# The first norm joined, reciprocals of the softmax sums turned, and three of eight low parts at the FFN heads moved to ScalarE and GpSimd

## The reference

```python
def rms_norm(x, g):
    xf = x.astype(jnp.float32)
    y = xf * lax.rsqrt(jnp.mean(xf * xf, axis=-1, keepdims=True) + EPS)
    return (y * g.astype(jnp.float32)).astype(x.dtype)

def sink_softmax(logits, sink):
    m = jnp.maximum(jnp.max(logits, axis=-1, keepdims=True), sink)
    p = jnp.exp(logits - m)
    return p / (jnp.sum(p, axis=-1, keepdims=True) + jnp.exp(sink - m))

def conv_ffn(x, left, g, w_gate, w_up, cw, cb, w_down):
    xn = rms_norm(x, g)
    a = xn @ w_gate
    ...
    y = (jax.nn.gelu(ac) * (xn @ w_up)) @ w_down
    return y, ap[:, -(CONV_W - 1):]

for i in range(DEPTH):
    ...
    hp = hp + op @ wo                       # mixer, then
    fp, cp = conv_ffn(...)                  # FFN
    hp = hp + fp[:, META:]
```

## Time and profile before

| | |
|---|---|
| median of 3 runs | 2940.51 us (2939.18 to 2941.53) |
| the profiled execution | 2940.25 us, of which 2938.4 are the span of its trace |
| granted TensorE clock, mean | 0.984 of full speed |
| busy, share of the span | PE 97%, PEld 91%, DVE 52%, ACT 23%, POOL 31% |
| first norm and projections of layer 0 | 22 to 174 us |
| attention of layer 0 | 176 to 374 us |
| head of the first FFN (norm m = 1) | 477 to 499 us |
| attention of layer 1 | 1633 to 1955 us |
| head of the second FFN (norm m = 3) | 2057 to 2079 us |

### The profile page before, as it was taken

How to read it: one execution, slowest core, us unless ns; L and a number is a source line. 1 busy time by engine, 2 the same in 40 slices (tenths; PEclk the granted TensorE clock), 3 DMA queues, 4 the chain that set the end, 5 groups by cost and what they waited for, 6 DMA issues and landing times. The chain is left out here.

```text
span 2938.4 us, 48132 instructions
## 1 busy us (share of the span) xinstructions
PE 2854.0 (97%) x18679; PEld 2687.3 (91%) x18679; DVE 1532.0 (52%) x2816; ACT 679.4 (23%) x1327; POOL 918.6 (31%) x860
## 2 busy tenths in 40 slices
PE   8999999999999999999888899999999999999998
PEld 6988899999999999998578777789999999999997
DVE  5046615554444444455588878531644444444455
ACT  4036611000000000003466655631100000000002
POOL 4233333222222222224024754323222222222221
PEclk9999999999999999999999999999999999999999
DMA  4430011111111111114012000011111111111112
GB/s 124 66 98 10 22 30 36 42 37 36 43 43 43 43 43 37 42 43 132 1 31 77 10 12 9 21 74 44 36 44 43 36 43 43 43 41 37 43 36 75
DMA packets 178206, 129.82 MB, mean 44 GB/s; under 512 B 25313, under 2 KB 168353, under 8 KB 177846
## 3 DMA queue, kind: packets, MB, share of 16 engines
q1 hardware_dynamic: 178066, 127.90, 15.4%
HBM read 111.13 MB, written 15.16 MB: 43 GB/s over the span
## 5 line engine op out<-in xcount | busy, mean ns | idle before, releaser
L1221 POOL CAST w_hi<-w_raw 128x1024 fp32r<-128x1024 f32 x120 | 145.2, 1210 | 1099.1 <-PE ps_gemm L1458 599.9
L668 DVE TENSOR_TENSOR h<-h,ps_gemm 128x1170 f32<-128x1170 f32 (+1 forms) x192 | 262.5, 1367 | 394.6 <-PE ps_gemm L1474 208.5
L1458 PE MATMUL ps_gemm<-xh,w_hi 128*128 128x390 f32 (+1 forms) x1920 | 445.8, 340 | 0.0
L1458 PE MATMUL ps_gemm<-xl,w_hi 128*128 128x390 f32 (+1 forms) x1920 | 444.9, 340 | 0.0
L1458 PE MATMUL ps_gemm<-xh,w_lo 128*128 128x390 f32 (+1 forms) x1920 | 444.7, 340 | 0.0
L1458 PEld LDWEIGHTS ps_gemm<-xh,w_hi 128*128 128x128 f32 x1920 | 349.2, 189 | 0.1
L1458 PEld LDWEIGHTS ps_gemm<-xl,w_hi 128*128 128x128 f32 x1920 | 348.1, 189 | 0.0
L1458 PEld LDWEIGHTS ps_gemm<-xh,w_lo 128*128 128x128 f32 x1920 | 348.0, 189 | 0.0
L1224 POOL TENSOR_TENSOR w_lo<-w_raw,w_hi 128x1024 fp32r<-128x1024 f32 x120 | 290.7, 2423 | 17.4
L676 ACT ACTIVATE ac<-ac 128x1184 f32<-128x1184 f32 x44 | 52.5, 1194 | 857.7 <-DVE ac L735 857.7
L1421 PE MATMUL ps_gemm<-xl,w_hi 128*128 128x390 f32 (+1 forms) x1056 | 246.2, 341 | 0.0
(11 more groups left out here) (412 smaller groups left out, 4705.7 us busy)
## 6 DMA issues: line engine op xcount, KB each, us to landing
w_raw<-in_w_gate SPq DMA_DIRECT2D x44, 512.0 KB, 3.8
w_raw<-in_w_up SPq DMA_DIRECT2D x44, 512.0 KB, 3.8
w_raw<-in_w_down SPq DMA_DIRECT2D x44, 512.0 KB, 3.5
w_raw<-in_w_in_b SPq DMA_DIRECT2D x13, 512.0 KB, 3.9
w_raw<-in_w_qkv_a SPq DMA_DIRECT2D x10, 512.0 KB, 3.9
residual_park<-h SPq DMA_DIRECT2D x1, 4680.0 KB, 13.7
h<-residual_park SPq DMA_DIRECT2D x8, 585.0 KB, 7.3
out<-yt SPq DMA_DIRECT2D x9, 512.0 KB
```

The lines of the kernel that those rows point to most:

```text
L668: dve.tensor_tensor(c3(h[:, m, :], l), c3(h[:, m, :], l), pse(j, l), ALU.add).then_inc(evac[j % 2], 1)
L1221: pool.tensor_copy(whi[c % 3][:], raw[c % 2][:]).then_inc(w_hi_done, 1)
L1458: mm = pe.matmul(ps[j % 2][:, m_, 0:ch], w[:, k, :], x[:, k, x0 + m_ * ch:x0 + (m_ + 1) * ch], start=(k == 0 and w is wh and x is XH), sto ...
```

## The change

**In the first norm** (m = 0) ScalarE makes all eight high parts and then all eight squares; VectorE makes all eight low parts and then adds all seven squares, those of GpSimd too; GpSimd adds none and goes on to the splits. The sum of the squares moves from behind the first product into the second, behind its 60th matmul (`between`, k = 6).

Three low parts came in, and one split moved behind them and the last add. The diff, cut to its core:

```diff
@@ gpsimd
+            def low_part(m, k):
+                pool.wait_ge(xh_done, 8 * m + k + 1)
+                pool.wait_ge(xl_raw, of_gpsimd(m, k))
+                pool.tensor_tensor(XL[:, k, :], x3["x_scaled"][:, k - SPLIT_LO, :], XH[:, k, :].bitcast(F32),
+                                   ALU.subtract).then_inc(xl_pool, 1)
@@ split_ffn
-                    if c in (c0 - 4, c0 - 2, c0, c0 + 2):
+                    if c in (c0 - 4, c0 - 2, c0):
                         add_one(m, c - c0 + 5)
+                    if c == c0 + 1:
+                        pool.wait_ge(mm_done, last_job(c0 - 1) + 1)
+                        for k in range(SPLIT_LO, KT):
+                            low_part(m, k)
+                        add_one(m, KT - 1)
@@ first splits
                 split(c)
-                if c == 0:
-                    add_squares(0)
@@ gemm, gated
-                        pe.wait_ge(xl_done, gate + k + 1)
+                        if k < low_of_dve(gate // KT):
+                            pe.wait_ge(xl_done, low_count(gate // KT, k))
+                        else:
+                            pe.wait_ge(xl_pool, of_gpsimd(gate // KT, k))
@@ transposes
-                        if b == "rinv":
+                        if b == "rinv" and i >= WIDE:
+                            pe.wait_ge(p_wide, wide(layer, i))
+                            mm = pe.transpose(tb[j % 2][:, P * k:P * (k + 1)],
+                                              inverse(layer, i).rearrange("p r d -> p (r d)"), ident[:])
+                        elif b == "rinv":
@@ first products
-                gemm(i, J_PA + i, XH, XL, n, gate=0 if i == 0 else None)
-                if i == 0:
-                    square_sum(0, G_X)
+                gemm(i, J_PA + i, XH, XL, n, gate=0 if i == 0 else None, between=squares_between if i == 1 else None)
@@ scalar, norm
+                if m == 0:
+                    for k in range(KT):
+                        high_part(k)
                 for k in range(KT):
...
-                    if m < 4:
-                        copy(XH[:, k, :], h[:, k, :], gT[:, k, NORM_G[m]:NORM_G[m] + 1]).then_inc(xh_done, 1)
+                    if 0 < m < 4:
+                        high_part(k)
+                    if m in (1, 3) and k == KT - 1:
+                        act.wait_ge(mm_done, j_prev)
+                        scaled_parts()
@@ scalar, prompt
+                def repeat_inverse(i):
+                    act.wait_ge(p_rinv, NU * layer + i + 1)
+                    if i >= WIDE + 2:
+                        act.wait_ge(p_tr, transposed(layer, i - 2))
+                    copy(inverse(layer, i), stat(2, i).unsqueeze(2).to_broadcast([P, 2, HD])).then_inc(p_wide, 1)
...
                     part(parts[1])
+                    if WIDE < n <= NU:
+                        repeat_inverse(n - 1)
                     if n < NU:
                         probs(n, 1)
@@ vector
-                if k and k % 2 == 0:
+                if k and (k % 2 == 0 or m == 0):
...
-                    for k in range(KT):
+                    for k in range(SPLIT_LO):
                         low_part(m, k)
                         if k == 2:
                             add_square(m, KT - 2)
...
+                        if n - 4 >= WIDE:
+                            dve.wait_ge(p_wide, wide(layer, n - 4))
                         dve.reciprocal(stat(2, n - 1), stat(1, n - 1)).then_inc(p_rinv, 1)
...
             for k in range(KT):
                 low_part(0, k)
+            for k in range(KT):
                 add_square(0, k)
```

More of the change, by code:

```diff
@@ L159, in build @@
         FULL = KT * T * 4
+        SPLIT_LO = 5
         rreg = region(4 * T + 56, [("rms_scale", [P, T], F32)],
@@ L180, in build @@
              ("sb_vc", [P, HD], F32), ("sb_v", [P, 2, HD], F32), ("kts_b", [P, 272], F32), ("qs_b", [P, P], F32),
-             ("ptb_h", [P, 512], F32)],
+             ("ptb_h", [P, 512], F32), ("ri_b", [P, 2, 2, HD], F32)],
             [("skip_scm2", [P, SCW], F32), ("skip_m02", [P, 416], F32), ("skip_sc2", [P, 288], F32),
@@ L210, in build @@
             [("gu_hi", [P, 2, T], F32R), ("gu_lo", [P, 2, T], F32R), ("ctx_rows", [18, D_FF], F32)],
+            [("skip_gu", [P, 5 * T - 16], F32), ("x_scaled", [P, KT - SPLIT_LO, T], F32)],
             [("rl2", [P, 1024], F32), ("rl3", [P, 1024], F32), ("kit_s", [P, DEC_BATCH, PAST], F32),
@@ L222, in build @@
             [("kt0", [P, T], F32), ("kt1", [P, T], F32), ("vf", [P, T], F32),
-             ("kts_a", [P, 2, 160], F32), ("sbias_a", [P, 2, 160], F32)],
+             ("kts_a", [P, 2, 160], F32), ("sbias_a", [P, 2, 160], F32), ("ri_a", [P, 2, 2, HD], F32)],
             [("skip_k", [P, 2 * T], F32), ("pta_v", [P, 2, 512], F32)],
@@ L259, in build, with low_of_dve, of_gpsimd, low_count @@
         xl_done = sem("x_lo_done")
+        xl_pool = sem("x_lo_of_gpsimd_done")
+        xl_raw = sem("x_scaled_for_gpsimd")
+        def low_of_dve(m):
+            return (KT, SPLIT_LO, KT, SPLIT_LO)[m]
+        def of_gpsimd(m, k):
+            return (0, 0, 0, 1)[m] * (KT - SPLIT_LO) + k - SPLIT_LO + 1
+        def low_count(m, k):
+            return sum(low_of_dve(i) for i in range(m)) + k + 1
         sq_done = sem("square_done")
@@ L518, in stat, with wide, inverse @@
             return rreg["stats"][:, o:o + 2] if r is None else rreg["stats"][:, o + r:o + r + 1]
+        WIDE = 16
+        def wide(layer, i):
+            return (NU - WIDE) * layer + i - WIDE + 1
+        def inverse(layer, i):
+            return (hreg["ri_b"] if layer else x4["ri_a"])[:, i % 2, :, :]
         def near_at(i):
@@ L628, in build @@
         p_rinv = sem("pair_row_sum_inverse_done")
+        p_wide = sem("pair_inverse_repeated")
         p_tr = sem("pair_probs_transposed")
@@ L1334, in set_masks_b @@
                 pool.wait_ge(sq_done, 24)
-                pool.wait_ge(xl_done, 24)
+                pool.wait_ge(xl_done, low_count(2, KT - 1))
                 pool.wait_ge(ix_sum, DEC_BATCH)
@@ L1648, in constants, with squares_between @@
                 pe.matmul(tb[g % 2][0:HEADS, 0:FLEN], x3["tab"][:], x3["bsel"][:], start=True, stop=True).then_inc(pe_tr, 1)
+            def squares_between(k):
+                if k == 6:
+                    square_sum(0, G_X)
             pe.wait_ge(dve_setup, 1)
             for i, (kind, _, n) in enumerate(proj_a):
-                gemm(i, J_PA + i, XH, XL, n, gate=0 if i == 0 else None)
-                if i == 0:
-                    square_sum(0, G_X)
+                gemm(i, J_PA + i, XH, XL, n, gate=0 if i == 0 else None, between=squares_between if i == 1 else None)
                 if i == 1:
@@ L2032, in norm, with high_part, scaled_parts @@
                     act.wait_ge(stores, 16 * 22)
+                def high_part(k):
+                    copy(XH[:, k, :], h[:, k, :], gT[:, k, NORM_G[m]:NORM_G[m] + 1]).then_inc(xh_done, 1)
+                def scaled_parts():
+                    for k in range(SPLIT_LO, KT):
+                        copy(x3["x_scaled"][:, k - SPLIT_LO, :], h[:, k, :], gT[:, k, NORM_G[m]:NORM_G[m] + 1]).then_inc(xl_raw, 1)
+                if m == 0:
+                    for k in range(KT):
+                        high_part(k)
                 for k in range(KT):
@@ L2181, in add_square @@
             def add_square(m, k):
-                if k and k % 2 == 0:
+                if k and (k % 2 == 0 or m == 0):
                     dve.wait_ge(sq_done, 8 * m + k + 1)
-                    dve.wait_ge(acc_done, 7 * m + k - 1)
-                    dve.tensor_tensor(x4["acc"][:], x4["acc"][:], x4["sq1"][:], ALU.add).then_inc(acc_done, 1)
+                    if k > 1:
+                        dve.wait_ge(acc_done, 7 * m + k - 1)
+                    dve.tensor_tensor(x4["acc"][:], x4["acc"][:], x4["sq1" if k % 2 == 0 else "sq0"][:], ALU.add).then_inc(acc_done, 1)
             def scale(m):
```

## The result

| | before | after |
|---|---|---|
| median | 2940.36 us (2939.18 to 2941.53, 4 runs) | 2921.72 us (2920.99 to 2923.4, 4 runs) |
| profiled execution, span | 2940.25, 2938.4 us | 2920.99, 2919.2 us |
| granted TensorE clock, mean | 0.984 | 0.986 |

The changed kernel is 18.6 us faster: ratio 0.9938 (95% interval 0.9922 to 0.9954). The forecast was 2937.0 with a range from 2929, so it was 15.3 us too high. Rival 2 named 2922, but its mechanism, a port that doesn't exclude, is not what happened.

What follows compares the result with a forecast made beforehand. TensorE was taken to bound the attention, products and then VectorE's low parts the FFN heads. From 2940.25 us, A -2.6, B -7.2 and C +6.6 gave 2937.0 us, range 2929 to 2944.

Steps and rivals of the forecast that it cites:

- Rival 2: FFN heads: VectorE and GpSimd don't exclude each other on the port; C is -8.4, total 2922; chance 0.06.
- A: First norm: high parts in one block, product two straight behind product one, product three earlier; -2.6 us, bounds -6.9 and +1.1.
- B: Attention, 57 of 73 units a layer: one turn replaces the reciprocal row's matmuls; 0.085 us a unit (0.01 to 0.16), -7.2.
- C: Two FFN heads: three low parts move to GpSimd, holding the shared port 2.65 us each; +6.6 us, bounds +9 and -8.
- the tie: FFN heads: GpSimd's first part or VectorE's third low part gets in first, +4.5 or +1.9; taken as 3.3 a head.
- the moved split: FFN heads: GpSimd's split behind its low parts and add is for the third product, over 13 us later, so covered.
- Rival 1: VectorE wins the tie at both heads and turns gain their full pitch, 0.11 us; total 2930.8; chance 0.24.
- the stand before it: First norm: TensorE stands up to 3 us ahead of the sum of squares inside product two.
- product three: First norm: TensorE's third product begins at 65.1 us instead of 68.90, 3.8 earlier.
- Rivals 3 and 4: 3: a turn after a wait costs 0.26, total 2943.1, chance 0.13; 4: clock falls in attention layers, 2949.8, chance 0.07.

Runs made afterwards that it cites:

- again: Second profile of the very same changed kernel, nothing changed; 2921.45 us, ratio 0.9937 to before.
- A alone: Kernel before with only the first-norm change joined, reciprocals and FFN heads as before; 2933.37 us, ratio 0.9977 to before.
- the last kernel: Changed kernel, but VectorE makes all low parts, GpSimd adds first, its split waits for them, in the first norm for added squares; 2914.17 us, ratio 0.9917 to before.

## Why the prediction was wrong

| step | forecast | by the stages of after (again) |
|---|---|---|
| A, first norm | -2.6 | -2.3 (-3.1), and -3.9 (-1.4) at the start of the attention |
| B, layer 0 | -4.8 | -6.1 (-6.1) |
| B, layer 1 | -2.4 | -5.1 (-5.1) |
| C, two heads | +6.6 | -0.4 (+1.5) |
| elsewhere | 0 | -1.3 (+0.3), index stage and final norm |

**C is the step that failed, 7 of the 15 us.** The term was mis-sized: "an engine that holds the shared port for 2.65 each" took the price of GpSimd's add for that of its subtraction. In the trace after, VectorE's low parts 3 and 4 start at 473.75 and at 477.10:

```profile
477.10 3.43 DVE L2245 SCALAR_TENSOR_TENSOR xl<-h,gains,xh 128x1170 fp32r<-128x1170 f32 x1
```

They stand 3.35 us apart, and the first three, which ran free, 1.35, so GpSimd's subtraction holds VectorE up for 2.00. The add's price had been read too high as well. Before, the low part that stood beside it was

```profile
487.52 3.83 DVE L2178 SCALAR_TENSOR_TENSOR xl<-h,gains,xh 128x1170 fp32r<-128x1170 f32 x1
```

and the next began at 491.27, so the add held VectorE up for 2.40; 2.65 came out because 1.31 instead of 1.35 was taken for a low part. Three times 0.65 is 2.0 a head. The rest is the tie, which I had called open and averaged: VectorE got in first at both heads, by 0.03 us; at the first:

```profile
469.04 1.43 DVE L2245 SCALAR_TENSOR_TENSOR xl<-h,gains,xh 128x1170 fp32r<-128x1170 f32 x1
```

and GpSimd's first part at 469.07. With VectorE first and 2.00, my own arithmetic (+1.9) comes to about nothing for the first head; measured was +0.4 at the sum of squares. At the second head a later tie, between VectorE's add and GpSimd's first part, made -0.9 or +0.4 of it, in two profiles of one kernel. That the engines exclude each other was right. The Trainium skill's rule (SBUF — State Buffer, "Who interferes with whom") has a VectorE instruction with two inputs in SBUF contend with a GpSimd instruction that reads SBUF; the trace agrees with the 3.35. The forecast took the lock to last for the whole instruction; here GpSimd's add, 2.65 us long where VectorE's parts were done (2057.46), held VectorE up for only 2.40 where they weren't. The step's other figures held: GpSimd asks 2.7 us behind the first low part, and the moved split is covered.

**B: a term of the right kind, mis-sized.** The gain of a unit is 0.108 us, not 0.085. Two readings were off and partly cancel: the turn costs 0.108 in a row, not the 0.185 of the middle of my bounds, and the row that it replaced was worth two turns, 0.216, not the 0.27 between two starts in the earlier trace rows. I went to the middle though the row is there a unit before TensorE wants it, so that the turn doesn't wait and the pitch applies. Rival 1 had 0.11, but by luck: it took the turn's pitch for the gain, and the forecast's own row less that pitch would have been 0.16. In layer 1 I took waits of 5.4 us in all at 15 units as a sign that half the units wait; the doubled turn shows that most don't, and the waits that there are didn't grow:

```profile
PEld ps_far L1937 <- DVE stats L2630: 5.1, 13, 1.3
```

ScalarE's copy cost next to nothing, as forecast.

**A: the mechanism was right, its number partly luck.** The sum of squares, the stand before it and product three are within 1.5 us. But product three came 1.0 earlier than forecast, and the fall of the clock behind it cost some 2.5 instead of the 1.2 that I charged; the two about cancel in the -2.3. (By the windows of the earlier trace rows the fall there had lasted 6.8 us, not 6.4.) What I left out is that an earlier or later stand can bring or spare a fall of the clock in the next stage; A alone was worth 6.4. This comes with A in nine of eleven profiles but is no work: again the same kernel got only 1.4 of the 3.9.

Rival 2's time came true for another reason: B's and A's gains, not a free port. Rivals 3 and 4 didn't occur: units gained, and the clock stood at 1.00 in the steady part of both layers (290 to 358, and 1690 to 1930).

## What to carry to other kernels

Price a hold on a shared port from a row of the same operation in the same situation (queued behind the other engine), from start to start of the engine that is held up, and add up the port's holds in order: that sum foretold the first head of the last kernel, with an add and no subtraction of GpSimd's in it, to 0.2 us. Where two engines ask within 0.03 us of each other, reckon with both orders. Work that nobody waits for, as a weight's split, must be kept off the port by a wait while the critical engine uses it; moving it in the queue alone can put it in a worse place. And where one profile of before and one of after differ in stages that the change doesn't touch, profile the same kernel twice before looking for a cause.

## What the hardware showed that was not expected

- GpSimd's subtraction of 128 x 1170 holds up VectorE for 2.00 us, its add of the same size for 2.40, though the add is 2.65 long by itself.
- VectorE's instruction with one input from SBUF (128 x 1170, fp32) and GpSimd's subtraction take turns as well: 2.82 and 2.78 long at one pitch of 2.74. Which inputs or outputs make them do so was not tried further.
- Two 64-column fp32 matmuls against the identity cost TensorE as much in a row as two 128 x 128 turns (0.108 us each).
- The same code had the final norm in 27.65 to 32.34 us, at a mean granted clock of 0.84 and 0.72.
